# Half of the cached value pages fetched from SyncE's queue instead of GpSimd's, in a fused RWKV-7, forgetting-attention and product-key expert step

## The reference, cut to what matters

```python
past_k = cache_k[l][page_table].reshape(n_seq, n_pages * PAGE_SIZE, B_HEADS, B_HEAD_DIM)
past_v = cache_v[l][page_table].reshape(n_seq, n_pages * PAGE_SIZE, B_HEADS, B_HEAD_DIM)
...
p = jax.nn.softmax(jnp.concatenate([s_past, s_new], axis=-1), axis=-1)
o = (jnp.einsum('bhqk,bkhd->bqhd', p[..., :p_len].astype(past_v.dtype), past_v)
     + jnp.einsum('bhqk,bkhd->bqhd', p[..., p_len:].astype(v.dtype), v))
```

## Time and profile before

| | |
|---|---|
| median of three runs | 2630.75 us (2624.63 to 2638.81) |
| span of the profiled execution | 2649.1 us |
| mean granted TensorE clock in it | 0.935 of 2.4 GHz |
| PE, DVE, POOL, ACT busy | 80%, 64%, 54%, 11% |
| DMA | 792 MB, 299 GB/s in the mean |
| PE in PRE, first to last value page | 544.7 to 623.3 us |
| PE in CHAIN | 623.6 to about 912 us |

### The profile page before, as it was taken

One profiled execution on the slowest core, in us unless ns is written; L12 is line 12 of the kernel. 1 busy time (PEld: TensorE's weight loads), 2 busy tenths in 40 slices (PEclk: granted clock), 3 DMA queues, 4 the chain that ended last, 5 costly groups with the idle time before them and its releaser, 6 DMA issues.

```text
span 2649.1 us, 31845 instructions
## 1 busy us (share of the span) xinstructions
PE 2107.4 (80%) x10266; PEld 864.1 (33%) x10266; DVE 1696.8 (64%) x3928; ACT 297.3 (11%) x645; POOL 1434.9 (54%) x1559
## 2 busy tenths in 40 slices
PE   4999999978888857688888678887767667767677
PEld 3444444524444447533233123332111111111111
DVE  2389998775533244857666686666777766777633
ACT  2112222311111110111100010100000000000000
POOL 0233332233333201477777776777777777777762
PEclk7899999889999978899999899899899999999998
DMA  7376776487555653899999999999999999999994
GB/s 264 128 254 229 258 253 208 160 302 239 190 169 186 205 171 112 298 385 390 403 402 372 361 375 372 379 396 370 377 360 370 344 337 376 352 352 369 365 368 160
DMA packets 264139, 792.05 MB, mean 299 GB/s; under 512 B 33208, under 2 KB 64668, under 8 KB 263480
## 3 DMA queue, kind: packets, MB, share of 16 engines
q0 software_dynamic: 191008, 680.63, 70.2%
q1 hardware_dynamic: 72992, 109.61, 12.0%
HBM read 779.03 MB, written 11.09 MB: 298 GB/s over the span
## 4 chain that ended last, share of the span: by engine, by line
POOL 38%; issue 15%; PE 2%; DMA 2%; another core or an unknown queue 1%; PEld 1%; DVE 0%; PEldq 0%; ACT 0%; POOLq 0%; ACTq 0%; DVEq 0%
POOL arena L881 38%; DMA arena<-in_peer_v,arena 2%; PE bank L1443 1%; PE bank L1417 0%; PEldq L1495 0%; PEld bank L1484 0%; PEld bank L1443 0%; PE bank L1426 0%; PE bank L1458 0%; DVE arena L2434 0%; DVE arena L2431 0%; PEld bank L1491 0%; DVE arena L2413 0%; DVE arena L2420 0%
## 5 line engine op out<-in xcount | busy, mean ns | idle before, releaser
L1443 PE MATMUL bank<-arena 128*32 128x512 f32 x2048 | 940.8, 630 | 329.0 <-DMA arena<-in_peer_v,arena 279.7
L2477 DVE CUSTOM_DVE_ANT_0 arena<-arena 128x1024 f32<-128x1024 f32 x512 | 624.4, 1222 | 378.5 <-DMA arena<-in_peer_u,arena 339.2
L881 POOL DMA_INDIRECT arena<-in_peer_u,arena x520 | 575.3, 1106 | 340.1 <-issue 153.5
L881 POOL DMA_INDIRECT arena<-in_peer_v,arena x520 | 582.7, 1121 | 223.4 <-issue 151.3
L1443 PEld LDWEIGHTS bank<-arena 128*32 128x32 f32 x2048 | 181.7, 112 | 1006.2 <-DMA arena<-in_peer_v,arena 541.1
L906 PE MATMUL bank<-arena 128*128 128x128 f32 (+8 forms) x1528 | 387.9, 410 | 38.6 <-DMA arena<-in_w_up_a 13.8
L864 POOL DMA_DIRECT2D arena<-in_cache_k x256 | 137.4, 537 | 351.5 <-issue 219.5
L1505 ACT ACTIVATE arena<-bank 128x512 f32<-128x512 f32 (+13 forms) x362 | 155.6, 430 | 1344.8 <-remote 235.5
L906 PEld LDWEIGHTS bank<-arena 128*128 128x128 f32 (+3 forms) x1528 | 241.7, 191 | 188.6 <-issue 145.6
L864 POOL DMA_DIRECT2D arena<-in_cache_v x256 | 137.3, 536 | 268.9 <-issue 168.8
L1888 DVE TENSOR_TENSOR arena<-arena 128x512 f32<-128x512 f32 x256 | 175.1, 684 | 67.9 <-ACT arena L1505 47.5
(11 more groups left out here) (283 smaller groups left out, 1707.6 us busy)
## 6 DMA issues: line engine op xcount, KB each, us to landing
arena<-in_cache_k POOLq DMA_DIRECT2D x256, 256.0 KB, 3.7
arena<-in_cache_v POOLq DMA_DIRECT2D x256, 256.0 KB, 4.0
arena<-in_w_ada SPq DMA_DIRECT2D x12, 2048.0 KB, 12.0
arena<-in_w_in SPq DMA_DIRECT2D x10, 2048.0 KB, 13.3
arena<-in_peer_wq SPq DMA_DIRECT2D x16, 1024.0 KB
arena<-in_peer_u,arena POOLq DMA_INDIRECT x520
arena<-in_peer_v,arena POOLq DMA_INDIRECT x520
arena<-in_w_o SPq DMA_DIRECT2D x8, 1024.0 KB, 10.4
```

The source lines that it names most:

```text
L881: nc.gpsimd.indirect_dma_start(gathered[:, j, :], None, tables[kind[0]][:, :], OFF(ap=index, axis=0)).then_inc(row_in[j], 16)
L1443: ins = mm(acc[u][32 * j:32 * (j + 1), :], spread[:, n % 2, b, :], gathered_row(("v", t, x))[:, 512 * u:512 * (u + 1)], start=x < 4, stop= ...
L2477: release(nc.vector.tensor_tensor_reduce(out=row, in0=row, in1=h2[:, t, :], scale=1.0, scalar=0.0, op0=MUL, op1=ADD, accum_out=gelu[:, at: ...
```

## The change

Of each round of eight value pages, POOL still issues the first four (slots 0 to 3). SP issues the last four (slots 4 to 7). SP reads the page numbers itself, from the same row, with indices that are constants. The page lands on one of four new semaphores, `value_in`, for which PE waits instead of `page_loaded`. The waits for free slots have the same values as POOL's had. Key pages stay with POOL. SP's fetches are written into its order of work at fixed places: round 0 ahead of the loop over j, round 1 behind the wait for SAMPLE's end at j = 2, round j at the end of each j from 2 to 7 (behind the weights of `an{j+2}`), rounds 8 to 17 behind the end of PRE, and rounds 18 to 31 behind the passage of the sample outputs through DRAM.

```diff
+        value_in = [sem(f"value_in{j}") for j in range(4, RING)]
...
             mod_bias(0)
             mod_bias(1)
-
+            ids = buf("ids_row")[0:1, :].bitcast(I32)
+            value_rows = cache_v.rearrange("l n s h d -> (l n) s (h d)")
+
+            def value_pages(first, last):
+
+                for r in range(first, last):
+                    four = [sp.value_load(ids[:, RING * r + 4 + i:RING * r + 5 + i], min_val=0, max_val=POOL - 1) for i in range(4)]
+                    for j, page in enumerate(four, 4):
+                        sp.wait_ge(page_free[j], NS * PAGES // RING + r + 1)
+                        load(pages[:, j, :], value_rows[ds(page, 1), :, :].rearrange("o p d -> (o p) d"), value_in[j - 4])
+
+            value_pages(0, 1)
             for j in range(8):
                 if j == 2:
                     sp.wait_ge(phase_end, 3 * (SAMPLE + 1))
+                    value_pages(1, 2)
                     load(buf("wkv"), state_wkv.rearrange("l b h (e i) j -> (l b h e) (i j)", e=2), state_in)
...
                 if j < 6:
                     weights(f"an{j + 2}")
                     mod_bias(j + 2)
+                if j >= 2:
+                    value_pages(j, j + 1)
 
             sp.wait_ge(phase_end, 3 * (PRE + 1))
+            value_pages(8, 18)
             sp.wait_ge(wkv_ready, 1)
...
             load(buf("so_rows")[0:8, :], scratch_o, so_in)
+            value_pages(18, 32)
             sp.wait_ge(stored, OUTPUTS[0])
...
-                        for half in range(0, RING, 4):
+                        for half in range(0, 4 if past else RING, 4):
...
-                    pe.wait_ge(page_loaded[j], 16 * (32 + 4 * n + pg // RING + 1))
+                    if j < 4:
+                        pe.wait_ge(page_loaded[j], 16 * (32 + 4 * n + pg // RING + 1))
+                    else:
+                        pe.wait_ge(value_in[j - 4], 16 * (4 * n + pg // RING + 1))
```

## The result

The changed kernel takes 2666.61 us in the median of nine runs (2647.33 to 2688.58), the kernel before in nine runs beside it 2634.48 us (2624.63 to 2648.84). The ratio is 1.0089, with a 95% interval from 1.0062 to 1.0116. That is **23 us slower**, where I forecast 2625 us, 6 us faster. The ratio leaves out the slowest run of the changed kernel, the one that its first profile fell on; the medians of all runs are 32 us apart. The time is just inside my range (2592 to 2667), and it is the case slower by over 0.5%, to which I had given 0.26.

What follows compares the result with a forecast made beforehand. CHAIN was taken to be held by POOL's issue time and PRE's end by the DMA engines. CHAIN -42, PRE +35 and small edits +1 gave -6 us, so 2625 us against the median of 2630.75, range 2592 to 2667.

Steps and rivals of the forecast that it cites:

- What bounds the kernel: CHAIN held by POOL's issue time, PRE's end by the DMA engines; shifts of CHAIN's end carry one for one.
- one small edit: In CHAIN, the passage of the sample outputs can hold back round 18 once: 0 to 4 us, taken as 1.
- PRE, forecast 35 us lost: SP's pages queue behind weights and SP's read of an{j}; PRE's pages end about 658 us instead of 623.3.
- The first mark: In PRE, round 1 fed by two queues gains 4 us, moving the mark from 561.7 to 557.7.
- The four cycles: In PRE, modulation to modulation for j = 2 to 5: 18.3 us each where they took 12.1, leading to 631.
- The last two rounds: PRE's end: SP's stores, loads, reads and issues from 631.5 us, pages landing in 2.8 us, ending about 658 us.
- The rival that PRE hardly suffers: Same bytes fill the same DMA engines, so PRE loses only 10 us; kernel at 2600 us, chance 0.22.
- CHAIN, forecast 42 us gained: POOL issues four pages per round of eight, SP the others beside it; bounds nothing to 55 us.
- the wait falls from 72.7 us to under 15: Sign in CHAIN: PE's page waits at L1161 shrink so far, with group pairs of about 61 us.
- The conversion: In CHAIN, 0.68 of PE's page wait counts as lost time (49 us), of which 85% comes back.
- The rival that SP is no better feeder: In CHAIN SP needs 2.5 us or more a page, so no gain while PRE loses; 2667 us, chance 0.18.
- The rule on queues: DMAs from several engines share 16 DMA engines; judged to fit PRE's end, not CHAIN, where sequencer time is short.

Runs made afterwards that it cites:

- e7: Kernel before, all value pages on POOL's queue, but page numbers taken from loop registers instead of read from the page table; ratio 0.9830, CHAIN 247.3 us.
- second look: Second profile, no edit, of the changed kernel (span 2669.2 us) and of the kernel before (2651.2 us); stages are read from these.
- c_after: The changed kernel profiled a second time, no edit; PRE 143.4 us, CHAIN 257.8 us.
- e1: Changed kernel with value-page rounds 18 to 23 also issued ahead of the passage of the sample outputs; ratio 1.0057, CHAIN 253.6 us.
- e4: Changed kernel with SP's pages of round j ahead of the weights of an{j+2}, still behind the read of an{j}; ratio 1.0024, PRE 125.1 us.
- e5: Changed kernel with SP's pages of round j issued at the head of step j, before the wait for an{j}; ratio 0.9911, PRE 95.6 us.
- e8: Changed kernel with e5's pages at the head of each step and e6's non-blocking passage; ratio 0.9880, PRE 96.3 us, CHAIN 251.5 us.
- c_before: The kernel before profiled a second time, no edit, for stage marks; PRE 93.1 us, CHAIN 285.3 us.
- e2: Changed kernel with SP issuing pages only from round 8 on, rounds 0 to 7 POOL's alone; ratio 0.9877, PRE 92.2 us, CHAIN 266.8 us.
- e3: Changed kernel with the edits of e1 and e2 together; ratio 0.9865, PRE 93.1 us, CHAIN 258.2 us.
- e6: e2 with the sample passage opened up: its load behind round 24, the 1 MB state store behind round 31; ratio 0.9906, CHAIN 252.0 us.
- e9: Kernel before with no value page fetched in CHAIN (rounds 8 to 31 left out, PE not waiting); ratio 0.9802, CHAIN 227.5 us.

## Why the prediction was wrong, point by point

**What bounds the kernel.** Right. CHAIN was held by POOL's issue time (e7), and what happened up to CHAIN's end was carried to the end of the kernel one for one (1737.3 and 1737.4 us behind it). The mechanisms were the ones on record. What failed were the sizes of two terms, PRE's loss and CHAIN's remaining wait, and one small edit, all to the same side.

**PRE, forecast 35 us lost, measured 50.** The 15 us lie in three places, counted from the start of PRE (531.0 in the prediction's profile, 530.68 in the second look).
- *The first mark*, 3.5 us: SP's stores of `an2` stood at 30.2 us (560.87 - 530.68) where I had put 26.7 (557.7 - 531.0). The 4 us that two queues were to gain in round 1 came as about 1.5: in the mean 29.0 us in c_after, e1, e4, e5 and e8, where SP takes part in round 1, and 30.5 us in the first profile of the kernel before, c_before, e2, e3, e6 and e9, where POOL reads and issues it alone. The rest is scatter (28.0 to 30.2 us among the five).
- *The four cycles*, 6 us: from there to the stores of the heads at 640.86 they took 80.0 us for 73.8. The first three, forecast as 18.3 us each, came as 19.4, 20.5 and 19.2. From the issue of the weights to the end of SP's pages on PE it was 14.7 to 15.2 us, where I had 14.2 (10.8, 2.1 and 1.3), and a modulation behind a standstill could be slower: `an4` took 2.62 us at a granted clock of 0.72, and 1.96 us at 1.00 in the second look at the kernel before (0.5 is 1.2 GHz, 1.0 is 2.4).
- *The last two rounds*, 5.6 us: 32.1 us from those stores to the end of the last page, for 26.5. The last round alone took 3.9 us more than forecast. Its pages were 5.2 us on the way in the median, where I had put 2.8, the shortest landing of the earlier trace rows.

```profile
597.13 2.62 PE L950 MATMUL bank<-arena 128*32 128x128 f32 x64 [0.26 <-issue]
...
562.50:575.00 12.50, 2.70 (x7) 0.43 (x8) 12.22 (x9) 0.00 (x0) 1.69 (x4) 0.71 0.93 337
581.70:594.00 12.30, 0.98 (x3) 0.22 (x4) 0.00 (x0) 0.00 (x0) 1.87 (x4) 0.63 0.91 340
```

The windows are those of the standstills. Their 337 and 340 GB/s in the mean do not say that the rate of 388 was wrong: the mean has the start in it, before the weights flow. In 40 slices of 581 to 594 us the DMA engines moved 372 to 422 GB/s from the eleventh to the last but one:

```profile
GB/s 14 14 14 14 0 101 126 309 315 359 384 403 410 403 397 422 416 422 372 397 403 391 385 378 378 372 410 378 391 378 372 391 403 385 397 378 372 385 403 265
```

How the loss splits I had not worked out; e4 and e5 show that 18 us were the weights ahead of the pages, 29.5 us SP's coming late, and 2.5 us stay.

**The rival that PRE hardly suffers** (0.22). False for this order, and true for the order of e5: the same bytes on the same queues cost 2.5 us more than before. My argument against it, the store held for 15.2 us, pointed the right way.

**CHAIN, forecast 42 us gained, measured 27.5.** Two steps failed. First, "the wait falls from 72.7 us to under 15": from 73.3 us it fell to 40.6 (the four idle times above), and even in e6, where the passage no longer holds SP up, to 32.3. I had let every wait end with POOL's issue time. Why so much of it stays is not shown; a page also takes 4 us to land, and the groups of pages come in bursts on a ring of eight slots. The conversion that I applied was too low, if anything. I took 0.68 of the wait and 85% of that, 0.58, and the changed kernel saved 27.5 us for 32.7 us less wait, 0.84 (e6: 33.3 for 41.0, 0.81). So the term was a wait wrongly taken to vanish, times a factor wrongly taken small. Second, the small edit (the passage holds back round 18 once, taken as 1 us) cost 6 to 7 us (69.5 us against 62.4 in its neighbours). SP stood from the state's store at 771.27 to its next pages at 785.56, first for DVE's `wkv_ready`, then for its own small store, then for four reads. The SP rows, the POOL row and the PE rows:

```profile
771.27 0.44 SPq L640 DMA_DIRECT2D out<-arena  x1
780.13 0.33 SPq L637 DMA_DIRECT2D scratch_out<-arena  x1
782.64 0.32 SPq L637 DMA_DIRECT2D arena<-scratch_out  x1
785.56 8.34 SPq L637 DMA_DIRECT2D arena<-in_cache_v  x8
```
```profile
772.83 1.73 POOL L881 DMA_DIRECT2D arena<-in_cache_v  x3 [3.57 <-PE bank L1181]
```
```profile
780.06 3.44 PE L1181 MATMUL bank<-arena 128*8 128x512 f32 x8 [1.01 <-DMA arena<-in_cache_v]
...
789.61 3.79 PE L1181 MATMUL bank<-arena 128*8 128x512 f32 x8 [2.44 <-DMA arena<-in_cache_v]
```

The second PE row is SP's half of round 18: PE waits 2.4 us, and the eight products take 3.8 us, where they take 1.05 when the pages are there. The first is POOL's half, issued from 772.83 us on, behind the 1 MB store at 771.27, and not there before 780. So the store may have had a part in it too, and how the 6 to 7 us divide between store and standstill is open. I had looked at what the passage itself costs (two DMAs) and not at the time that SP waits ahead of it for DVE while slots 4 to 7 lie free.

**The rival that SP is no better feeder** (0.18). False by its mechanism: between the load at 782.64 and the next page issue at 785.56 SP needed 2.6 us for four reads, POOL's price, and four issues took 1.96 us. So a round cost SP 4.6 us where I had 4.2. That the measured time lies beside this rival's 2667 us is a coincidence, since CHAIN did gain.

**The rule on queues.** The Trainium skill (DMA: Bandwidth & Descriptors, section Issuing engines are not separate DMA queues) says that starting DMAs on more engines saves only the sequencer's time to start them. By that rule e7 agrees: the saving can be had on one queue, by shortening what the sequencer does between issues. Where I weighed it I was right that it does not speak against CHAIN's gain. It does speak against moving pages in PRE, where the sequencer's time was not what was short.

**The sum.** -42 + 35 + 1 became, by the marks, -33 + 50 + 6 = +23 us. The three errors of 9, 15 and 5 us add up because all lie on one side. In a difference of two terms of 40 us that is enough to turn the sign.

**Left open.** What keeps the last 20 to 25 us between e6 or e7 and e9. The rows show that PE still waits for pages in e6 (32 us), with landings of about 4 us in CHAIN, and that it costs less with one queue and no reads. Landing time, bursts, the number of slots and what is left of issue time were not told apart, and more slots were not tried. In the two-queue versions that are faster than before, e2, e3, e5, e6 and e8, the ratios from 0.9865 to 0.9911 are not told apart by their intervals.

## What to carry to other kernels

When work moves to a queue that has a written order of its own, its price is set by its place there: list every wait that stands ahead of each moved piece, and who will be idle while the queue stands in it. Here the same split cost 50 us or 2.5 us in one phase by the position of two lines, and a wait that had cost nothing cost 6 us once pages stood behind it. When the sum is a small difference of large terms, take the median landing and not the shortest, and do not put a remaining wait at zero without a row that says so: here over half of it stayed.

## What the runs showed of the hardware

Four page numbers read from SBUF into registers cost SP 2.6 us, as they cost POOL, although the reads themselves are short in the records of the changed kernel:

```profile
L721 SPq TENSOR_LOAD <-arena x128: 260/267/688, 507.3 to 911.2; - x128
L721 SPq FUSED_REGOPS  x128: 147/152/181, 507.9 to 911.5; - x128
L721 SPq SEQ_ASSERT  x128: 18/18/33, 508.1 to 911.7; - x128
```

The three records of a read add up to 0.44 us in the median, 1.7 us for four, so about 0.9 us of the 2.6 are in no record. The floor of about 600 ns that the prediction quotes for a tensor load does not hold for these records (260 ns and more); the whole read, 0.65 us, lies above it. And pages on SP's queue did not land sooner than on POOL's in this order of work: in CHAIN 4.4 us in the median against 4.0 us (96 and 92 pages of the changed kernel), over the whole kernel 4.7 against 4.2 us.
